# A two-layer decoder trunk on one core: low-part products last in each weight quarter, and the first norm's factors multiplied into turned rows

## The reference

```python
def rms_norm(x, gain):
    y = xf * lax.rsqrt(jnp.mean(xf * xf, axis=-1, keepdims=True) + EPS)
    return (y * gain.astype(jnp.float32)).astype(x.dtype)

def even_mixer(xn, pos, lb, w_in, hgrn_gain, w_out):
    h = jnp.einsum('bsd,de->bse', xn, w_in)        # w_in is 1024 x 8192
    ...
    f = lbb + (1.0 - lbb) * jax.nn.sigmoid(to_chunks(f_logit))
```

## Time and profile before

| | |
|---|---|
| median of 3 runs | 611.58 us (611.43 to 611.94) |
| the profiled execution: its time, its span | 611.41 us, 609.6 us |
| TensorE busy | 589.8 us, 97% |
| VectorE busy | 420.3 us, 69% |
| ScalarE busy | 382.4 us, 63% |
| GpSimd busy | 65.2 us, 11% |
| DMA | 97.83 MB, mean 160 GB/s |
| granted TensorE clock, mean | 0.993 |

### The profile page before, as it was taken

One profiled execution on the slowest core, in us unless ns is written; L12 is line 12 of the kernel. 1 busy time (PEld: TensorE's weight loads), 2 busy tenths in 40 slices (PEclk: granted clock), 3 DMA queues, 4 the chain that ended last, 5 costly groups with the idle time before them and its releaser, 6 DMA issues.

```text
span 609.6 us, 9739 instructions
## 1 busy us (share of the span) xinstructions
PE 589.8 (97%) x3913; PEld 540.7 (89%) x3913; DVE 420.3 (69%) x625; ACT 382.4 (63%) x571; POOL 65.2 (11%) x60
## 2 busy tenths in 40 slices
PE   8699999999999999999999999999999999999985
PEld 7689989999899989889988999999899998888964
DVE  3598759725985796476664876598996963766654
ACT  6385478256546757457656665859938837566762
POOL 6703001300100100100000000304110100100000
PEclk9799999999999999999999999999999999999999
DMA  9554445736454446436442833334553454256101
GB/s 289 161 187 139 139 140 162 242 101 220 127 186 138 140 154 230 169 138 212 163 178 61 286 139 139 139 139 152 203 199 139 155 217 151 100 211 237 69 2 69
DMA packets 51836, 97.83 MB, mean 160 GB/s; under 512 B 1356, under 2 KB 7760, under 8 KB 51792
## 3 DMA queue, kind: packets, MB, share of 16 engines
q1 hardware_dynamic: 51248, 96.87, 46.9%
q10 hardware_dynamic: 160, 0.27, 0.1%
q0 software_dynamic: 384, 0.08, 0.1%
HBM read 96.16 MB, written 1.05 MB: 159 GB/s over the span
## 4 chain that ended last, share of the span: by engine, by line
PE 70%; ACT 10%; DVE 9%; DVEq 4%; issue 3%; POOL 2%; ACTq 2%; POOLq 0%
PE proj L1676 11%; PE proj L1677 11%; PE proj L1678 11%; PE proj L1695 9%; PE proj L1697 9%; PE proj L1696 9%; DVE w_lo L1023 4%; PE head L1833 3%; ACT w_hi L465 3%; PE head L1922 1%; POOL prm_rows L360 1%; ACT xT_hi L487 1%; DVE work L1296 1%; ACT junk L473 1%; ACT work L854 1%
## 5 line engine op out<-in xcount | busy, mean ns | idle before, releaser
L1023 DVE TENSOR_TENSOR w_lo<-raw_weights,w_hi 128x1024 fp32r<-128x1024 f32 x174 | 223.8, 1299 | 128.9 <-ACT w_hi L465 126.7
L465 ACT ACTIVATE w_hi<-raw_weights 128x1024 fp32r<-128x1024 f32 x176 | 184.6, 1057 | 118.0 <-PE proj L1678 54.9
L1676 PE MATMUL proj<-xT_hi,w_hi 128*128 128x256 f32 x736 | 212.7, 289 | 0.7 <-DVE xT_lo L1047 0.7
L1677 PE MATMUL proj<-xT_lo,w_hi 128*128 128x256 f32 x736 | 208.2, 283 | 0.0
L1678 PE MATMUL proj<-xT_hi,w_lo 128*128 128x256 f32 x736 | 208.1, 283 | 0.0
L1676 PEld LDWEIGHTS proj<-xT_hi,w_hi 128*128 128x128 f32 x736 | 141.0, 192 | 2.7 <-issue 2.4
L1677 PEld LDWEIGHTS proj<-xT_lo,w_hi 128*128 128x128 f32 x736 | 141.1, 192 | 1.0 <-issue 0.7
L1678 PEld LDWEIGHTS proj<-xT_hi,w_lo 128*128 128x128 f32 x736 | 141.0, 192 | 0.0
L1695 PE MATMUL proj<-w_hi,y_hi 128*128 128x512 f32 x200 | 79.5, 397 | 0.0
L1697 PE MATMUL proj<-w_lo,y_hi 128*128 128x512 f32 x200 | 77.9, 390 | 0.0
L1696 PE MATMUL proj<-w_hi,y_lo 128*128 128x512 f32 x200 | 77.9, 389 | 0.0
(11 more groups left out here) (274 smaller groups left out, 752.2 us busy)
## 6 DMA issues: line engine op xcount, KB each, us to landing
raw_weights<-in_ev_w_in_dram SPq DMA_DIRECT2D x15, 2048.0 KB, 9.7
raw_weights<-in_od_w_in_dram SPq DMA_DIRECT2D x12, 2048.0 KB, 8.0
raw_weights<-in_ev_w_out_dram SPq DMA_DIRECT2D x4, 2048.0 KB, 7.8
raw_weights<-in_xa_wkv_dram SPq DMA_DIRECT2D x4, 2048.0 KB, 7.8
raw_weights<-in_od_w_out_dram SPq DMA_DIRECT2D x4, 2048.0 KB, 7.7
raw_weights<-in_xa_wq_dram SPq DMA_DIRECT2D x2, 2048.0 KB, 9.3
raw_weights<-in_xa_wo_dram SPq DMA_DIRECT2D x2, 2048.0 KB, 8.2
raw_weights<-in_ev_w_in_dram SPq DMA_DIRECT2D x4, 512.0 KB, 7.4
```

The lines of the kernel that those rows point to most:

```text
L465: act.activation(ring_quarter(w_hi, n, q), raw_quarter(n, q), ACT.Copy).then_inc(hi_ready, 1)
L1023: dve.tensor_tensor(ring_quarter(w_lo, n, q), raw_quarter(n, q), ring_quarter(w_hi, n, q).bitcast(F32), ALU.subtract).then_inc(lo_ready, 1)
L1676: pe.matmul(dst, wh[:, k, :], x_hi[:, k, :], start=(k == 0), stop=False)
L1677: pe.matmul(dst, wh[:, k, :], x_lo[:, k, :], start=False, stop=False)
```

## The change

In each quarter the high-weight products of all k come first, then a wait for the low part, then the low-weight products. At the start GpSimd makes the low part of the first quarter (`first_low`) instead of the second's, directly behind its first mask; its four memsets go to VectorE; VectorE makes the low parts of the second and third. The factor product moves behind the third quarter. `first_rows` and the second turn go: VectorE multiplies `rstd_row` into the four `head` banks that still hold the turned raw x (`scale_turned`), one bank at a time between its other work, and xT_high and xT_low read them as before. ScalarE's order in the first quarters changes a little.

```diff
@@ -350,6 +351,12 @@
             pool.drain().then_inc(masks_ready, 1)
+            def first_low():
+
+                pool.wait_ge(hi_ready, 1)
+                pool.tensor_tensor(ring_quarter(w_lo, 0, 0), raw_quarter(0, 0), ring_quarter(w_hi, 0, 0).bitcast(F32),
+                                   ALU.subtract).then_inc(first_lo, 1)
+
             for name, rows in PARAM_ROWS[1:]:
@@ -358,18 +365,14 @@
                 pool.dma_start(prm_rows[r - P * t:r - P * t + rows, t, :], src).then_inc(prm_landed, 16)
-            pool.memset(seen_f[:], 1.0)
-            pool.memset(scan_mask[:], 1.0)
-            pool.memset(att[:], 0.0)
-            pool.drain()
-            pool.memset(scan_mask[:].rearrange("p (c s) -> p c s", s=HGRN_CHUNK)[:, :, 0:1], 0.0)
+            pool.wait_ge(masks_filled, 1)
             for c in (0, 2 * P):
...
             pool.tensor_copy(seen[:], seen_f[:]).then_inc(masks_ready, 1)
-            pool.memset(causal[:], 0.0)
+            first_low()
             pool.iota(dist[:, 0:S], pattern=[[1, S]], base=0, channel_multiplier=-1,
@@ -418,24 +421,6 @@
-            def second_low():
-
-                pool.wait_ge(hi_ready, 2)
-                pool.tensor_tensor(ring_quarter(w_lo, 0, 1), raw_quarter(0, 1), ring_quarter(w_hi, 0, 1).bitcast(F32),
-                                   ALU.subtract).then_inc(second_lo, 1)
-
-            def first_rows():
-
-                pool.wait_ge(rstd_ready, 1)
-                for c in range(2):
-                    for t in range(T):
-                        last = pool.tensor_scalar(mem_rows[:, t, 512 * c:512 * c + 512],
-                                                  x_sb[:, t, 512 * c:512 * c + 512], st[:, 6 + t:7 + t], None,
-                                                  ALU.mult)
-                    last.then_inc(normed, 1)
-
-            second_low()
-            first_rows()
             keys_carried(0)
@@ -545,11 +530,11 @@
             act.activation(prm[:, 0:KC], proj[2][:, 0:KC], ACT.Copy).then_inc(prm_ready, 1)
+            act.drain()
+            raw_high(range(0, 2))
             ahead(-1, 1)
-            act.drain()
-            raw_high(range(0, 4))
+            raw_high(range(2, 8))
             ahead(-1, 2)
-            raw_high(range(4, 8))
             ahead(-1, 3)
@@ -1072,7 +1057,13 @@
             dve.memset(st[:, 2:4], 0.0)
+            dve.memset(seen_f[:], 1.0)
+            dve.memset(causal[:], 0.0)
+            dve.memset(scan_mask[:], 1.0)
+            dve.memset(att[:], 0.0)
             dve.drain()
+            dve.memset(scan_mask[:].rearrange("p (c s) -> p c s", s=HGRN_CHUNK)[:, :, 0:1], 0.0)
+            dve.drain().then_inc(masks_filled, 1)
             def raw_low(ks):
@@ -1081,14 +1072,14 @@
-            ahead(-1, 1)
             dve.wait_ge(prm_ready, 1)
...
-            dve.wait_ge(second_lo, 1)
-            dve.wait_ge(hi_ready, 3)
-            dve.tensor_tensor(ring_quarter(w_lo, 0, 2), raw_quarter(0, 2), ring_quarter(w_hi, 0, 2).bitcast(F32),
+            dve.wait_ge(first_lo, 1)
+            dve.wait_ge(hi_ready, 2)
+            dve.tensor_tensor(ring_quarter(w_lo, 0, 1), raw_quarter(0, 1), ring_quarter(w_hi, 0, 1).bitcast(F32),
                               ALU.subtract).then_inc(lo_ready, 2)
+            ahead(-1, 3)
             rstd(0)
@@ -1200,6 +1191,12 @@
+            def scale_turned(b):
+
+                dve.wait_ge(rstd_copied, 1)
+                two = head[b][:].rearrange("p (k t) -> p k t", k=2)
+                dve.tensor_tensor(two, two, memT[:, 4:5, :].broadcast_to([P, 2, S]), ALU.mult).then_inc(turned, 1)
+
             def scaled_f(f, u):
@@ -1219,13 +1216,17 @@
                 else:
+                    scaled_f(f, 0)
                     ahead(f, 1)
-                    scaled_f(f, 0)
+                    scale_turned(0)
                     ahead(f, 2)
                     forget(g, 0)
+                    scale_turned(1)
                     ahead(f, 3)
                     scaled_f(f, 1)
+                    scale_turned(2)
                     ahead(i, 0)
+                    scale_turned(3)
                 forget(g, 1)
@@ -1236,8 +1237,6 @@
                 dve.wait_ge(lnf_ready, g + 1)
-                if g == 0:
-                    dve.wait_ge(masks_ready, 2)
                 dve.tensor_tensor_scan(wview(2), scan_mask[:], wview(0), 0.0, ALU.mult, ALU.add)
@@ -1278,6 +1277,8 @@
                 ahead(z, 1)
+                if g == 0:
+                    dve.wait_ge(masks_ready, 2)
                 for h in range(4):
@@ -1644,8 +1645,11 @@
                 pe.wait_ge(hi_ready, 4 * n + q + 1)
-                if (n, q) == (0, 1):
-                    pe.wait_ge(second_lo, 1)
+                pe.wait_ge(lo_ready, 4 * n + q + 1)
+
+            def low_ready(n, q):
+                if (n, q) == (0, 0):
+                    pe.wait_ge(first_lo, 1)
                 else:
@@ -1665,7 +1669,7 @@
                         take_bank(n, u)
-                split_ready(n, q)
+                pe.wait_ge(hi_ready, 4 * n + q + 1)
                 dst = bank(n, u, half)[:, col:col + S]
@@ -1675,6 +1679,8 @@
                     pe.matmul(dst, wh[:, k, :], x_lo[:, k, :], start=False, stop=False)
+                low_ready(n, q)
+                for k in ks:
                     last = pe.matmul(dst, wl[:, k, :], x_hi[:, k, :], start=False, stop=(k == KC - 1))
@@ -1694,6 +1700,11 @@
                         pe.matmul(dst, x_lo[:, k0 + k, tok], wh[:, k, :], start=False, stop=False)
+                low_ready(n, q)
+                for t in range(T):
+                    dst = bank(n, t, half)[:]
+                    tok = slice(P * t, P * t + P)
+                    for k in range(2):
                         last = pe.matmul(dst, x_hi[:, k0 + k, tok], wl[:, k, :], start=False, stop=final and k == 1)
@@ -1729,7 +1740,7 @@
                     if k % 4 == 0:
-                        pe.wait_ge(normed, 2 * norm + k // 4 + 1)
+                        pe.wait_ge(normed, 2 * norm + k // 4 - 1)
                     for t in range(T):
@@ -1765,10 +1776,10 @@
                              ).then_inc(prm_turned, 1)
+                slab_f(n, [2], x=(y_hi, y_lo))
                 pe.wait_ge(diag_ready, 1)
                 pe.matmul(proj[3][:, 0:S], avg[:], memT[:, 5, :], start=True, stop=True).then_inc(rstd_psum, 1)
-                slab_f(n, [2, 3], x=(y_hi, y_lo))
-                turn_rows(mem_rows, 0)
+                slab_f(n, [3], x=(y_hi, y_lo))
                 pe.wait_ge(prm_ready, 2)
```

More of the change, by code:

```diff
@@ L155, in hybrid_trunk @@
         out_landed = sem("out_landed")
+        masks_filled = sem("masks_filled")
         masks_ready = sem("masks_ready")
@@ L168, in hybrid_trunk @@
         raw_lo_ready = sem("raw_lo_ready")
-        second_lo = sem("second_lo")
+        first_lo = sem("first_lo")
         diag_ready = sem("diag_ready")
```

## The result

| | before | after |
|---|---|---|
| median of four runs | 611.6 us (611.43 to 611.94) | 615.82 us (615.59 to 616.66) |
| ratio to before | | 1.0073, 95% interval 1.006 to 1.0085 |
| profiled execution: time, span | 611.41, 609.6 | 615.96, 614.2 |
| TensorE, GpSimd busy | 589.8, 65.2 us | 592.1, 57.2 us |

A forecast was written before the change was run, and what follows sets the result against it. The prediction took TensorE, 97% busy, as the bound, with VectorE's chain to the decayed queries arriving together with it at 59.29. Terms: 611.4 + 0.7 - 0.5 + 2.4 = 614.0 us, range 609.5 to 616.8.

The forecast's parts named there:

- The bound and the drain: Start: GpSimd's drain waits for its own DMAs until 14.1, so TensorE's stall is 3.7 us instead of 5.7.
- the short drain: Rival at the start: drain belongs to the long memsets, low part ready at 12.1, no stall; 610.2 us, chance 0.24.
- The clock: Start: TensorE's granted clock stays at 1.00 around the 3.7 us stall, factor product at 24.4.
- A stall two thirds as long: Argument against a clock fall in the first quarter: TensorE stands 3.7 us, where it stood 5.7.
- the clock falls as well: Rival at the start: after the stall 24 products run slow, costing 2.2 us; 616.2 us, chance 0.20.
- The factors in the banks: VectorE between 29.3 and 44: four bank products of 0.62 us, +2.5 less idle times of 0.28 and 0.44.
- The moved memsets: Start: four memsets, 2.7 us, go to VectorE, which has nothing to do until the first w_hi; cost nothing.
- Low products last: All other quarters: -0.5 us from TensorE's wait at 429, against +2.4 in three quarters after norms.
- The paced quarters: Three first quarters after later norms, paced by VectorE's xT_low: low products behind the last step cost +0.8 each, +2.4 us.
- Sum: Whole run: 611.4 + 0.7 (start and chain to L1810) - 0.5 + 2.4 = 614.0 us, chance 0.44.
- nearly 10 us: TensorE's claimed saving at the start, from stall, slow clock, transposes and order, lost again in later waits.
- TensorE sets the pace: Rival at the start: VectorE's chain has more room, whole saving near 9.8 us shows; 603.5 us, chance 0.05.

The follow-up runs named there:

- the kernel before with early low part: Kernel before, with GpSimd making the second quarter's low part directly behind its DMA issues, ahead of its memsets and drain: 610.65 us, ratio 0.9994.
- The filled stalls: Changed kernel plus unread identity products, 16 ahead of the first low products and 11 ahead of the decayed queries' products: 612.93 us, ratio 1.0027.
- the early low part: Changed kernel with GpSimd's first low part moved directly behind its DMA issues, ahead of masks and drain: 609.09 us, ratio 0.9969.
- the early low part turned twice: Changed kernel with the first low part ahead of masks and drain, bank multiplications replaced by GpSimd's first_rows and the second turn: 609.75 us, ratio 0.9965.
- the kernel with interleaved quarters: Changed kernel, but in the four first quarters after a norm each low product again follows its two high products: 613.32 us, ratio 1.0028.

## Why the prediction was right, and where it was not

**The bound and the drain: right.** The drain ends at 14.3 (forecast "about 14"), the low part starts at 14.82 (14.6), the stall is 3.90 (3.7). It was argued from one coincidence, a drain end 0.5 behind a landing, with the short drain at a chance of 0.24. Four profiles now show the end at 14.07, 14.26, 14.52 and 14.05 with last landings at 13.54, 13.73, 13.99 and 13.51, while what stands ahead of the drain differed, and with the DMAs elsewhere it took 0.6 us. Eight more profiles of these kernels say the same: in all twelve the end lies 0.53 or 0.54 behind the last landing. In the kernel before with early low part the drain ended at 17.28, behind its memsets, with the last landing long over at 13.68. That "Perfetto Trace Analysis" of the Trainium skill, DMA Instruction — SWDGE (GPSIMD), lets the profile end such a DMA with its descriptors is no contradiction: the interval ends there, but the drain waits on.

**The clock: the step that failed.** "A stall two thirds as long" was taken as a reason against a fall. The clock fell at 17.16 and came back at 20.57. The rival "the clock falls as well" (0.20) was the true case, but at another price: 24 products in 2.2 us were reckoned, some 16 ran slow, and the factor product came 1.6 late, at 25.96 and not 24.4. Of this 1.0 reached the decayed queries. That 616.2 is so near to 615.8 is luck: another 1.6 us are a **second fall**, at 61.5, behind the longer wait at L1821, which no part of the prediction had. The filled stalls show both together at 2.9 us of median, and with them the kernel takes 612.9, where the forecast said 614.0. So the forecast was 2.9 short by the clock and 1.1 too high by the rest, and that it lies only 1.8 off owes something to luck.

**The factors in the banks: right in kind, too dear.** 0.62 times four was right within 0.1. But 1.76 net was forecast and the stretch from the chain's first instruction (29.30, now 29.65) to the scan grew from 14.69 to 16.06, 1.37: VectorE had about 0.35 us of further idle time, in gaps that carry no mark. L1810 was to come at 60.0 and came at 60.99: 1.56 by the factor product, less 0.4 here, less 0.1 ahead of it. The moved memsets cost nothing, as reckoned: they end at 4.7 on VectorE, which does nothing more until 8.16.

**Low products last.** The paced quarters were forecast at +2.4 and measured +2.5 by the profile and by the median of the kernel without them: right. The gain was -0.5 and is -1.2: besides the 0.48 of idle time marked at 429 there were smaller gaps that carry no mark, at 429 itself, at the same place of the next quarter but one, 5.7 us later, and at 528, and they went too. At 168 the wait grew from 0.40 to 1.21, as expected.

**Sum.** Forecast +0.7 - 0.5 + 2.4 = 2.6; measured +1.7 - 1.2 + 2.5 + 1.6 = 4.6. Of the four terms three are within 1.0, and the largest miss is a term that was not there.

**Two readings that were wrong.** TensorE was to save "nearly 10 us" at the start and to stand idle for 8 or so between 35 and 60. The terms named for it sum to 2.0 + 1.9 + 1.9 = 5.8. Measured, TensorE began the second slab 3.7 us earlier (29.70, before 33.43) and was idle for 4.0 us from 35 to 60.99. The forecast didn't use the number, but the rival "TensorE sets the pace" was priced with it, and 603.5 was too low by some 4 us. And not all other waits of TensorE were under 1.5 us: one of 1.8 stands at the very start, the same in both kernels.

**The other side.** "Drain short" was priced at 610.2, and the early low part, which gives the start that this rival described, takes 609.09. The mechanism was right; only the trigger wasn't in this kernel. What no step saw is that the kernel before could not have used it. The same early low part gives the changed kernel 6.7 us and the kernel before 0.7 at most, not told from none, since there GpSimd's rows come onto the path. The bank multiplications, a loss of 1.0 to 1.4 us by themselves, take the rows away altogether; moving the memsets to VectorE and leaving the factor product behind the third quarter was enough as well, as the early low part turned twice shows.

## What to carry to other kernels

Before work is put behind GpSimd's next drain, look whether GpSimd has DMAs of its own in flight: put what others wait for ahead of the drain, or issue the DMAs elsewhere. When a long stall is shortened, ask what was hidden under it, and ask of every remaining stall of some 2 us or more on TensorE what the products behind it cost at the lower clock (the shortest one here with a fall behind it was 1.94); a few unread products there cost nothing, as long as the wait is there; where it wasn't, they cost 2.4 us. Where a producer paces TensorE step by step, keep the dependent products in its shadow: moved behind the last step they are paid in full.

## What the runs showed of the hardware that was not expected

- A GpSimd drain lasts until the DMAs that GpSimd issued have landed, 0.53 or 0.54 us behind the last of them in twelve profiles: 7.0 us in the changed kernel with them, 0.6 without. Where GpSimd's own work ahead of it ended later, it lasted until then (17.28).
- Behind waits of TensorE of 2.58 to 2.60 us the clock fell to half in three profiles and not in four. Among executions of one kernel, by their mean clocks, it fell in some and not in others (six of twelve for the early low part). Where it fell there it stayed down for 3.4 us. It fell for 3.4 us behind a single wait of 1.94 too. With the first stall of the changed kernel, 3.9 us, it was down for 3.4 us, and with the same stall in the kernel with interleaved quarters, 4.5 us there, for 6.8.
- GpSimd's two selects of 128x128 took 2.00 us at 17.85, beside two VectorE low parts (17.25 and 18.39), and 0.54 to 0.59 where VectorE stood idle or worked on small tiles. Its four rows operations took 6.6, 7.0, 8.6 and 9.1 us in four kernels; the two long ones ran beside four VectorE low parts each, the two short ones beside one. "SBUF — State Buffer" of the Trainium skill, Who interferes with whom, says that a VectorE instruction with two SBUF inputs contends with a GpSimd instruction that reads SBUF; the low parts are such, and the trace agrees. The reverse didn't show: these VectorE low parts took 1.21 to 1.31.
